# Normalising the attention probabilities on GpSimd instead of VectorE in a two-block fp32 kernel

## The reference, cut to what matters

```
DILATED_PATTERNS = ((128, 1), (512, 4), (2048, 16))
...
    s = jnp.einsum('bhrnqd,bhrnkd->bhrnqk', qb, kw) * (Dh ** -0.5)
    s = s - slopes[None, :, None, None, None, None] * (dist * dilation).astype(jnp.float32)
    s = jnp.where(valid[None, None, None], s, NEG_INF)
    m = jnp.max(s, axis=-1)
    p = jnp.exp(s - m[..., None])
    l = jnp.sum(p, axis=-1)
    o = jnp.einsum('bhrnqk,bhrnkd->bhrnqd', p, vw) / l[..., None]
...
    m_all = jnp.max(jnp.stack([m for (_, m, _) in outs]), axis=0)
    alphas = [l * jnp.exp(m - m_all) for (_, m, l) in outs]
    num = sum(a[..., None] * o for a, (o, _, _) in zip(alphas, outs))
    o = num / sum(alphas)[..., None]
```

## Time and profile before

| quantity | value |
| --- | --- |
| runs | 2541.58, 2545.62 and 2547.19 us, median 2545.62 us |
| profiled execution, from the first to the last instruction (its own time; no other is given) | 2551.3 us |
| TensorE busy | 98% of the span |
| VectorE, ScalarE, GpSimd busy | 44%, 29%, 21% |
| stretch of the attention | about 1659 to 2258 us |
| chain that ended last | TensorE 96% of the span, VectorE 2% |

### The profile page before, as it was taken

The page is one execution under the profiler, slowest core; times in us unless marked ns, Lnnn a source line. Parts: engine busy times, 40 slices in busy tenths (PEclk is TensorE's granted clock), DMA queues, the critical chain, the costliest instruction groups (busy, mean ns, idle before and its releaser), DMA issues.

```text
span 2551.3 us, 30196 instructions
## 1 busy us (share of the span) xinstructions
PE 2495.6 (98%) x11552; PEld 2045.1 (80%) x11552; DVE 1124.3 (44%) x1459; ACT 729.6 (29%) x1010; POOL 528.6 (21%) x231
## 2 busy tenths in 40 slices
PE   8999999999999999999999999999999999999997
PEld 6887888888888888887888888878778777778886
DVE  4424574333113311346322111377777777753434
ACT  4411122211111111124311101245555555541112
POOL 2121122122222222222222122211211212112212
PEclk9998899999999999999999999999999999999998
DMA  3110121111111111112222224233223323334222
GB/s 126 42 42 28 48 90 48 44 49 49 42 49 49 49 50 42 48 58 66 99 98 84 76 89 139 91 108 116 92 83 113 97 84 107 107 134 145 92 99 107
DMA packets 57484, 202.85 MB, mean 80 GB/s; under 512 B 6976, under 2 KB 7120, under 8 KB 57424
## 3 DMA queue, kind: packets, MB, share of 16 engines
q1 hardware_dynamic: 47056, 164.25, 20.3%
q10 hardware_dynamic: 10368, 37.75, 3.6%
HBM read 160.03 MB, written 41.94 MB: 79 GB/s over the span
## 4 chain that ended last, share of the span: by engine, by line
PE 96%; DVE 2%; issue 1%; DMA 1%; ACT 0%; DVEq 0%; SPq 0%; ACTq 0%
PE dense L551 28%; PE dense L552 28%; PE dense L553 28%; PE aux L784 2%; PE aux L768 1%; PE aux L769 1%; PE aux L797 1%; PE aux L796 1%; PE aux L659 1%; PE aux L656 1%; PE aux L731 1%; PE aux L581 0%; DVE att_p_lo L1535 0%; DMA residual<-kept_ya 0%; PE aux L573 0%
## 5 line engine op out<-in xcount | busy, mean ns | idle before, releaser
L551 PE MATMUL dense<-x_hi,w_hi 128*128 128x512 f32 x2512 | 1011.9, 403 | 16.6 <-DVE x_lo L1195 14.9
L552 PE MATMUL dense<-x_lo,w_hi 128*128 128x512 f32 x2512 | 985.3, 392 | 0.0
L553 PE MATMUL dense<-x_hi,w_lo 128*128 128x512 f32 x2512 | 985.2, 392 | 0.0
L468 POOL TENSOR_TENSOR w_lo<-w_raw,w_hi 128x1024 fp32r<-128x1024 f32 x197 | 475.0, 2411 | 1795.5 <-ACT w_hi L856 1795.5
L856 ACT CAST w_hi<-w_raw 128x1024 fp32r<-128x1024 f32 x197 | 207.2, 1052 | 1252.2 <-PE dense L553 1236.2
L551 PEld LDWEIGHTS dense<-x_hi,w_hi 128*128 128x128 f32 x2512 | 476.1, 190 | 109.6 <-issue 17.3
L553 PEld LDWEIGHTS dense<-x_hi,w_lo 128*128 128x128 f32 x2512 | 475.0, 189 | 102.3
L552 PEld LDWEIGHTS dense<-x_lo,w_hi 128*128 128x128 f32 x2512 | 476.6, 190 | 87.9 <-issue 1.2
L1236 DVE TENSOR_TENSOR work<-dense,rstd 128x1024 f32<-128x1024 f32 x135 | 165.0, 1222 | 722.6 <-PE dense L553 716.5
L551 PE MATMUL dense<-m_hi,w_hi 128*128 128x512 f32 x480 | 189.3, 394 | 0.2 <-DVE m_lo L1407 0.2
L552 PE MATMUL dense<-m_lo,w_hi 128*128 128x512 f32 x480 | 189.3, 394 | 0.0
(11 more groups left out here) (186 smaller groups left out, 2152.2 us busy)
## 6 DMA issues: line engine op xcount, KB each, us to landing
w_raw<-weights SPq DMA_DIRECT2D x197, 512.0 KB, 3.5
kept_qkv<-work ACTq DMA_DIRECT2D x24, 512.0 KB, 2.7
residual<-xT SPq DMA_DIRECT2D x16, 512.0 KB, 6.5
att_q<-kept_qkv SPq DMA_DIRECT2D x32, 256.0 KB, 4.1
att_k<-kept_qkv SPq DMA_DIRECT2D x32, 256.0 KB, 5.0
kept_x<-residual ACTq DMA_DIRECT2D x8, 512.0 KB, 2.7
att_v<-kept_qkv SPq DMA_DIRECT2D x8, 512.0 KB, 3.4
kept_mixed<-work ACTq DMA_DIRECT2D x8, 512.0 KB, 4.3
```

The source lines that it names most:

```text
L468: pool.tensor_tensor(WL[:, u.slot], WR[:, u.slot], WH[:, u.slot].bitcast(f32), ALU.subtract).then_inc(w_lo, 1)
L551: pe.matmul(dst, WH[:, u.slot, k], hi, start=(k == 0), stop=False)
L552: pe.matmul(dst, WH[:, u.slot, k], lo, start=False, stop=False)
L553: last = pe.matmul(dst, WL[:, u.slot, k], hi, start=False, stop=(k == nk - 1))
```

## The change

The multiplication of each block of probabilities by its reciprocal leaves VectorE and is issued on GpSimd, in place, behind what GpSimd has in that stage already. VectorE keeps the reciprocal. Before it overwrites a reciprocal, VectorE now waits for GpSimd to have used the one of the stage before (`pn`). `head_bias` waits for the last `ttr` of its stage. The two `sem_inc(turns, 1)` only separate waits.

```
@@ gpsimd, stage(pair, m)
                     pool.wait_ge(mx_in, pair.count(16, 16))
                     pool.tensor_tensor(MXL[:], MXL[:], WK[:, 14], ALU.mult).then_inc(ya_up, 1)
+                for b in range(4):
+                    p = PBS[m % 2][:, b, 0:(4 * (m % 2) + b + 1) * P]
+                    pool.wait_ge(rl, pair.count(16, 4 * m + b + 1))
+                    pool.sem_inc(turns, 1)
+                    pool.tensor_scalar(p, p, STAT[:, 3, b:b + 1], None, ALU.mult).then_inc(pn, 1)
@@ vector, normed(pair, m, b)
-                sb = m % 2
-                p = PBS[sb][:, b, 0:(4 * sb + b + 1) * P]
                 n = pair.count(16, 4 * m + b + 1)
                 dve.wait_ge(ex, n)
+                if m or pair.reg is not None or pair.off:
+                    dve.wait_ge(pn, pair.count(16, 4 * m + b - 3))
                 dve.reciprocal(STAT[:, 3, b:b + 1], STAT[:, 2, b:b + 1]).then_inc(rl, 1)
-                dve.wait_ge(rl, n)
-                dve.tensor_scalar(p, p, STAT[:, 3, b:b + 1], None, ALU.mult).then_inc(pn, 1)
@@ vector, stage
                     elif kind == "b":
+                        dve.wait_ge(ttr, pair.count(24, steps_before(m) + 8))
+                        dve.sem_inc(turns, 1)
                         head_bias(*after(pair, m))
```

## The result

The changed kernel takes 2625.93 us (median of 4 runs, 2619.68 to 2628.97) against 2546.4 us before (median of 4 runs, 2541.58 to 2553.36) on the same chip. The ratio is 1.0311, with a 95% interval of 1.029 to 1.0332. The forecast was 2540.5 us with a range of 2527 to 2572. It was wrong, and on the other side.

What follows compares the result with a forecast made beforehand. TensorE, busy 98%, was taken as the bound. With the old waits (26.9 us) gone and new ones added, stage 1 lost 5.8 us and stage 3 gained 10.9: 2545.6 - 5.1 = 2540.5 us, range 2527 to 2572.

Steps and rivals of the forecast that it cites:

- What bounds the kernel: TensorE, busy 98% of the span; its 16 odd-stage waits before a piece of scores for `biased` total 24.5 us.
- what the change removes: In odd stages n0 leaves VectorE, so l0 and r3 come earlier and both waits per pair go: -26.9 us.
- the delay of s5: Piece of scores s5 started 2.0 us late in stage 1 and 1.36 us late in stage 3; 26.9 us over 8 pairs.
- the other three multiplications: A stage's multiplications besides n0 lie beside TensorE's work; removing them from VectorE is worth nothing by itself.
- Even stages cost nothing: n3, 512 wide, starts at 1858.50 and t0 comes at 1864.58; six microseconds cover any price.
- The price of a block: GpSimd's tensor_scalar taken at the affine select's 1.07 ns an element; an odd stage's four blocks take 3.55 us.
- The low part of the queries taking a turn of 1.22 us: In stage 1 this VectorE instruction runs between two GpSimd blocks, adding 1.22 us to the 6.2 us before t0.
- rule of alternation: When VectorE and GpSimd both have work queued, the one that waits goes next; read from one instance near 1224 us.
- the wait that was forecast: Ahead of t0 in stage 1: 6.2 us of work in 3.46 us of room, a new wait of 2.7 us.
- (C): Rival: blocks cost as much as the two-input product, 7.8 us in odd stages; +57 us, 2603 us; chance 0.11.
- (B): Rival: GpSimd's tensor_scalar slower than its select, 1.7 ns an element; +20 to +30 us, 2566 to 2576; chance 0.16.

## Why the prediction was wrong

**What bounds the kernel** and **what the change removes** were right. The 16 waits were n0 held behind `w_lo`, and they vanished. The term was undersized: 26.9 us forecast, about 35 measured without the multiplication. The forecast took only the delay of s5 and called the other three multiplications worthless. They aren't quite: n0's move alone gave 28 us and leaving out the others 7 more, of which some 4 are the delay at o3 of stage 1, behind n2 and `head_bias`.

**Even stages cost nothing**: right, shown by the run with these alone. n3 took 1.57 us on GpSimd, within the six that it had.

**The price of a block** is the step that failed. "I take the affine select, 1.07 ns, since it too reads one tensor and writes one." It was 2.51 ns an element and 0.28 us for each instruction, above even the upper bound of the two-input product, so that four blocks cost 9.5 us and not 3.55. The likeness that was used, how many tensors are read and written, doesn't set the cost: one and two operations read and write the same and take 2.85 and 1.12 us.

**The clock** had no term in the sum. Behind the new waits TensorE ran at its lower level, which cost some 28 us in the changed kernel by the distances from t0 to t2. Some 20 us came back when the waits of stage 1 were filled.

**The low part of the queries taking a turn of 1.22 us**: wrong beside the one-operation blocks, where it ran at its usual length, and roughly right beside two-operation ones, where it took 1.74 and held a block for 1.0. One instance was too little to build a rule of alternation on.

**The agreement of the two-operation run is in part luck.** Its form costs what the forecast had assumed, and it had the wait that was forecast (2.8 us against 2.7) and none in stage 3. But from the product's end to t0 it was 5.8 us and not 6.2, and there was room for 3.0 and not 3.46, and these two cancel. Its time, 2548.7 us, is 8 above the forecast of 2540.5: the gain of 35 us is larger than the 26.9, but the slower clock behind the wait of stage 1 (0.51 granted for 2.87 us in the pair at 1835) takes back some 11, by the same measure from t0 to t2. The places were modelled well, the price was wrong, and the clock and the wait of o3 were missing.

**The rivals.** (C), the price of the two-input product, had a chance of 0.11 and was the nearest to what came. It gave waits of 7.0 and 3.5 us; measured were 7.65 and 2.98. That is close in part by luck, since its blocks cost 7.8 us and not 9.5, and it counted a turn for the queries that wasn't taken. It gave +57 us and left out TensorE's clock, and its time of 2603 lay outside the range. (B) had named 4.2 us for the four blocks as the point from which it turns slower, and the two-operation run, whose four blocks cost some 3.8 us undisturbed (1.12 for 1024 and 0.48 for 256 give 0.83 ns an element and 0.27 us each), came out level with the kernel before.

## What to carry to other kernels

When an operation is moved to an engine on which the trace doesn't show it, a range of 2.5 between the nearest rows is not a detail: measure the exact form first, since the same multiplication of 1024 elements costs 2.85 or 1.12 us on GpSimd depending on whether one or two operations are written. When a multiplication is slow because it meets another engine's instruction, look for a place in its own engine's list where it doesn't meet it, before moving it: one word of a list gave a ratio of 0.989 (0.9873 to 0.9906) here. And price a new TensorE wait of several us with the slower clock behind it.

## What the runs showed that was not expected

- One-operation tensor_scalar on GpSimd: 2.85 us for 1024 float32 elements and 0.92 for 256, by a column, multiply or add, and 2.77 and 0.85 by a constant. Two operations in one instruction: 1.12 and 0.48 us. A copy takes 1.04, a tensor_tensor with a spread column 1.89, one with two full inputs 2.4. Why the lesser form is the slower isn't known from these runs.
- VectorE's products with two inputs in SBUF grew by 0.80 us beside GpSimd's tensor_scalar of either form and by 1.58 beside its tensor_tensor, not by the whole length of the other's instruction. The low part of the queries, on 64 partitions, kept 1.22 us beside one-operation blocks and took 1.74 beside two-operation ones. Which part of an instruction excludes the other wasn't tried.
- The slower clock came behind short waits too, but not behind all: in the changed kernel the matmuls from 1907.8 to 1911 us, behind the 2.98 us wait of stage 3, start 0.43 us apart instead of 0.23, and behind two other waits of the same length nothing is slower. With two operations the waits of 2.8 us in stage 1 were followed by it in seven of eight pairs.
